# S5 stage of a two-layer decoder: output weights completed by a transfer that adds, in place of two GpSimd differences

## The reference

```python
lam_bar = exp(lam * dt)                        # one complex number per group and state
b_bar   = (lam_bar - 1) / lam * (b_re + i b_im)
bu      = b_bar applied to 16 channels of u     # per group, 64 states
states[t] = lam_bar * states[t-1] + bu[t]       # over the 512 tokens
y[t]    = Re(states[t]) . c_re - Im(states[t]) . c_im
z       = gelu(y + d * u) @ w_glu + b_glu       # then h += val * sigmoid(gate)
```

## Time and profile before

| | |
|---|---|
| Median of 3 runs | 1032.54 us (1030.46 to 1032.89) |
| Profiled execution, its own time | 1030.94 us |
| Its span | 1029.2 us (1.7 us lie around it) |
| PE busy | 1000.4 us, 97% of the span |
| DVE busy | 828.3 us, 80% |
| ACT busy | 477.1 us, 46% |
| POOL busy | 306.5 us, 30% |
| S5 stage | about 0 to 84.85 us, where TensorE's first GLU product starts |

### The profile page before, as it was taken

The page is one execution under the profiler, slowest core; times in us unless marked ns, Lnnn a source line. Parts: engine busy times, 40 slices in busy tenths (PEclk is TensorE's granted clock), DMA queues, the critical chain, the costliest instruction groups (busy, mean ns, idle before and its releaser), DMA issues.

```text
span 1029.2 us, 16636 instructions
## 1 busy us (share of the span) xinstructions
PE 1000.4 (97%) x5850; PEld 824.2 (80%) x5850; DVE 828.3 (80%) x1147; ACT 477.1 (46%) x872; POOL 306.5 (30%) x256
## 2 busy tenths in 40 slices
PE   9889999999999999999999999998999999999996
PEld 4677888888888888888887766886888888888886
DVE  7993588798898988995985777788898888989845
ACT  7863323444455344543413888236355354544421
POOL 8996887300000000031957320770000000001150
PEclk9899999999999999999999999998999999999999
DMA  6123434122322322230333110241322322234012
GB/s 253 37 44 130 139 106 143 62 91 101 136 75 88 111 113 102 82 123 1 123 128 103 43 61 1 82 163 60 104 82 82 132 92 102 82 104 160 22 42 82
DMA packets 31878, 97.53 MB, mean 95 GB/s; under 512 B 10696, under 2 KB 13256, under 8 KB 27984
## 3 DMA queue, kind: packets, MB, share of 16 engines
q1 hardware_dynamic: 31824, 96.83, 26.8%
HBM read 92.36 MB, written 2.10 MB: 92 GB/s over the span
## 4 chain that ended last, share of the span: by engine, by line
PE 78%; DVE 14%; issue 3%; ACT 2%; POOL 1%; POOLq 0%; DVEq 0%; ACTq 0%
PE ps L1744 17%; PE ps L1747 9%; PE ps L1765 8%; PE ps L1766 8%; PE ps L1767 8%; PE ps L1704 5%; PE ps L1705 5%; PE ps L1706 5%; DVE act L1069 3%; PE ps L1650 1%; PE ps L1652 1%; PE ps L1651 1%; PE ps L1937 1%; PE ps L1912 1%; PE ps L1924 1%
## 5 line engine op out<-in xcount | busy, mean ns | idle before, releaser
L448 POOL TENSOR_TENSOR gate_sb<-gate_sb 128x1 f32<-128x1 f32 x60 | 23.4, 390 | 688.0 <-DMA raw<-panels_in 508.3
L537 POOL TENSOR_TENSOR w_lo<-raw,w_hi 128x1024 fp32r<-128x1024 f32 x60 | 149.4, 2490 | 5.0
L1766 PE MATMUL ps<-hid,w_hi 128*128 128x512 f32 x384 | 150.5, 392 | 0.0
L1765 PE MATMUL ps<-hid,w_hi 128*128 128x512 f32 x384 | 150.4, 392 | 0.0
L1767 PE MATMUL ps<-hid,w_lo 128*128 128x512 f32 x384 | 149.6, 390 | 0.0
L700 ACT ACTIVATE s_hi<-w_raw 128x1024 fp32r<-128x1024 f32 (+1 forms) x104 | 87.8, 844 | 100.1 <-PE ps L1747 93.7
L1744 PE MATMUL ps<-hid,s_hi 128*128 128x512 f32 x448 | 121.3, 392 | 0.6 <-ACT acc L764 0.6
L1704 PE MATMUL ps<-hid,w_hi 128*128 128x512 f32 x304 | 120.4, 396 | 0.0
L1705 PE MATMUL ps<-hid,w_hi 128*128 128x512 f32 x304 | 118.6, 390 | 0.0
L1706 PE MATMUL ps<-hid,w_lo 128*128 128x512 f32 x304 | 118.5, 390 | 0.0
L1179 DVE TENSOR_TENSOR s_lo<-w_raw,s_hi 128x1024 fp32r<-128x1024 f32 (+1 forms) x104 | 101.8, 990 | 18.0 <-ACT s_hi L700 10.6
(11 more groups left out here) (272 smaller groups left out, 2052.4 us busy)
## 6 DMA issues: line engine op xcount, KB each, us to landing
raw<-panels_in SPq DMA_DIRECT2D x108, 512.0 KB, 3.3
w_raw<-pairs_in SPq DMA_DIRECT2D x28, 1024.0 KB, 5.4
xy<-xu_in SPq DMA_DIRECT2D x4, 512.0 KB, 8.1
out<-h SPq DMA_DIRECT2D x8, 256.0 KB, 2.1
prm<-prm_in SPq DMA_DIRECT2D x1, 1280.0 KB, 6.4
h<-x_rows_in SPq DMA_DIRECT2D x1, 1280.0 KB, 13.4
h<-x_rows_in SPq DMA_DIRECT2D x1, 768.0 KB, 7.0
dd<-dd_in SPq DMA_DIRECT2D x1, 256.0 KB, 6.3
```

The lines of the kernel that those rows point to most:

```text
L537: nc.gpsimd.tensor_tensor(w_lo[:, s, :], raw[:, s % 2, :], w_hi[:, s, :].bitcast(F32), ALU.subtract).then_inc(w_split, 1)
L1765: mm(to, w_hi[:, s, w], hid[:, 0, 0, HK * par + k, :], start=(k == 0), stop=False)
L1766: mm(to, w_hi[:, s, w], hid[:, 0, 1, HK * par + k, :], start=False, stop=False)
```

## The change

The real part of `w_ri` was `c_sum*l_re - c_im*l_sum`, the imaginary part `c_re*l_dif - c_sum*l_re`. Now the signs of `l_sum` and `l_dif` are chosen so that both parts are a sum with the same term `c_sum*l_re`, and the imaginary part is negated everywhere (in `w_ri`, `p_ri`, and the rotations of `run_states`). GpSimd writes two of the products straight into `w_ri` and the common one into `w_add` (2 buffers, with zeros at lag 0). Then one transfer, issued from GpSimd with an accumulate operation, adds `w_add` to both parts of `w_ri`, lag 0 included. The product `k_both` goes from VectorE to GpSimd, where `project(o)` makes it along with `k_im`.

```diff
-        w_mul = sb("w_mul", [P, 3, OGP, J + 1, C], where=early)
+        w_add = sb("w_add", [P, 2, OGP, J + 1, C], where=early)
...
-        k_both = sb("k_both", [P, OGP, J, C], where=early)
+        k_both = sb("k_both", [P, 2, OGP, J, C], where=early)
...
             def weights_mul(o, parts=range(3)):
 
-                wait(pool, w_done, 2 * o)
-                factors = ((c_sum, l_re), (PR("c_re"), l_dif), (PR("c_im"), l_sum))
+                wait(pool, y_mm, o - 2)
+                wait(pool, w_done, 16 * (o - 1))
+                w = w_ri[o % 3]
+                factors = ((w_add[:, o % 2], c_sum, l_re), (w[:, 1], PR("c_re"), l_dif), (w[:, 0], PR("c_im"), l_sum))
                 for i in parts:
...
             def weights_sum(o):
+
                 pool.wait_ge(w_part, 3 * o + 3)
-                wait(pool, y_mm, o - 2)
-                for ri, (a, b) in enumerate(((0, 2), (1, 0))):
-                    tt(w_ri[o % 3][:, ri, :, 1:].rearrange("p g j c -> p g (j c)"),
-                       w_mul[:, a, :, 1:].rearrange("p g j c -> p g (j c)"),
-                       w_mul[:, b, :, 1:].rearrange("p g j c -> p g (j c)"), sub).then_inc(w_done, 1)
-
-            def project_im(o):
+                wait(pool, w_lag0, 2 * o + 2)
+                wait(pool, w_done, 16 * o)
+                if o < 2:
+                    wait(pool, zeroed, 5 + o)
+                nc.gpsimd.dma_start(w_ri[o % 3][:].rearrange("p r g j c -> p r (g j c)"),
+                                    w_add[:, o % 2].rearrange("p g j c -> p (g j c)").unsqueeze(1)
+                                    .to_broadcast([P, 2, OGP * (J + 1) * C]), accum_op=add).then_inc(w_done, 16)
+
+            def project(o):
+
                 wait(pool, p_done, 2 * o - 2)
-                tt(k_im[:, o % 2], octet(PR("b_re"), o).unsqueeze(2).to_broadcast([P, OGP, J, C]),
-                   x_dif[:, pairs_of(o), :].unsqueeze(3).to_broadcast([P, OGP, J, C]), mul).then_inc(k_part, 1)
+                for t, b, x in ((k_both, "b_im", x_sum), (k_im, "b_re", x_dif)):
+                    tt(t[:, o % 2], octet(PR(b), o).unsqueeze(2).to_broadcast([P, OGP, J, C]),
+                       x[:, pairs_of(o), :].unsqueeze(3).to_broadcast([P, OGP, J, C]), mul).then_inc(k_part, 1)
...
             weights_mul(0, (0,))
             wait(pool, setup_v, SETUP_X)
-            project_im(0)
-            project_im(1)
+            project(0)
             weights_mul(0, (1, 2))
+            project(1)
             weights_sum(0)
             wait(pool, setup_a, SETUP_RSTD)
             inputs(0)
+            weights_mul(1)
             wait(pool, s_dd, 16)
             tt(dd[:, 0], dd[:, 0], dd[:, 1], mul).then_inc(setup_p, 1)
-            weights_mul(1)
             weights_sum(1)
...
-            for o in range(3, NO):
-                project_im(o)
+            for o in range(2, NO):
+                project(o)
                 weights_mul(o)
+                inputs(o)
                 weights_sum(o)
-                inputs(o)
...
-                    act_fn(w_ri[o % 3][:, ri, :, 0, :], octet(PR(c), o), ACT.Copy, scale=1.0 - 2.0 * ri).then_inc(w_lag0, 1)
+                    act_fn(w_ri[o % 3][:, ri, :, 0, :], octet(PR(c), o), ACT.Copy).then_inc(w_lag0, 1)
...
-                tt(k_both[:], octet(PR("b_im"), o).unsqueeze(2).to_broadcast([P, OGP, J, C]),
-                   xsum_ps[:, pairs_of(o), :].unsqueeze(3).to_broadcast([P, OGP, J, C]), mul).then_inc(p_part, 1)
...
             def project_sum(o):
                 q = o % 2
-                v.wait_ge(p_part, 2 * o + 2)
-                v.wait_ge(k_part, o + 1)
+                v.wait_ge(p_part, o + 1)
+                v.wait_ge(k_part, 2 * o + 2)
...
             def lags(o):
 
-                wait(pe, w_done, 2 * o + 2)
+                wait(pe, w_done, 16 * o + 16)
```

More of the change, by code:

```diff
@@ L154, in build @@
         sb("slots_hi", [P, 2, D], where=early)
-        w_mul = sb("w_mul", [P, 3, OGP, J + 1, C], where=early)
+        w_add = sb("w_add", [P, 2, OGP, J + 1, C], where=early)
+        sb("slots_mid", [P, OGP * (J + 1) * C], where=early)
         turn_k = sb("turn_k", [8, L], where=early)
         turn_t = sb("turn_t", [8, L], where=early)
-        sb("slots_lo", [P, 4 * D - 3 * OGP * (J + 1) * C - 2 * L], where=early)
+        sb("slots_lo", [P, 4 * D - 3 * OGP * (J + 1) * C - 3 * L], where=early)
         k_im = sb("k_im", [P, 2, OGP, J, C], where=early)
-        k_both = sb("k_both", [P, OGP, J, C], where=early)
+        k_both = sb("k_both", [P, 2, OGP, J, C], where=early)
         rs = sb("rs", [P, 2, OGP, NK], where=early)
@@ L207, in build @@
         x_dif = sb("x_dif", [P, GP, J], where=s5)
+        x_sum = sb("x_sum", [P, GP, J], where=s5)
         rstd_u = sb("rstd_u", [P, 2, NK], where=s5)
@@ L324, in build @@
         tanh_ps = ps[:, 4, 288:352].rearrange("p (n g) -> p n g", g=GP)
-        xsum_ps, xre_ps = (ps[:, 5, a:a + GP * J].rearrange("p (g n) -> p g n", n=J) for a in (0, 256))
+        xre_ps = ps[:, 5, 256:256 + GP * J].rearrange("p (g n) -> p g n", n=J)
         ident, ones = C_("ident"), C_("ones")
@@ L452, in weights_mul @@
             def weights_mul(o, parts=range(3)):
[L454 to L455 removed]
+                wait(pool, y_mm, o - 2)
+                wait(pool, w_done, 16 * (o - 1))
+                w = w_ri[o % 3]
+                factors = ((w_add[:, o % 2], c_sum, l_re), (w[:, 1], PR("c_re"), l_dif), (w[:, 0], PR("c_im"), l_sum))
                 for i in parts:
[L457 to L458 removed]
+                    to, c, l = factors[i]
+                    tt(to[:, :, 1:], octet(c, o).unsqueeze(2).to_broadcast([P, OGP, J, C]),
                        l[:, pairs_of(o), 1:].unsqueeze(3).to_broadcast([P, OGP, J, C]), mul).then_inc(w_part, 1)
@@ L484, in _ @@
             nc.gpsimd.memset(decay[:, :, 0:1], 0.0).then_inc(zeroed, 1)
+            for i in range(2):
+                nc.gpsimd.memset(w_add[:, i, :, 0], 0.0).then_inc(zeroed, 1)
             wait(pool, setup_v, SETUP_INV)
@@ L515, in _ @@
             nc.gpsimd.tensor_scalar(minus[:], ident, -1.0, 0.0, mul, add).then_inc(negated, 1)
-            project_im(2)
-            weights_mul(2)
-            weights_sum(2)
-            inputs(2)
-            for o in range(3, NO):
-                project_im(o)
+            for o in range(2, NO):
+                project(o)
                 weights_mul(o)
+                inputs(o)
                 weights_sum(o)
-                inputs(o)
-            wait(pool, w_done, 2 * NO)
             def split(u):
@@ L541, in _ @@
             split(1)
+            wait(pool, w_done, 16 * NO)
             wait(pool, p_done, 2 * NO)
@@ L918, in _ @@
             link(tt(l_re[:], cos_l[:], mag_ps, mul))
-            link(tt(l_sum[:], l_re[:], lim_ps, add))
-            link(tt(l_dif[:], l_re[:], lim_ps, sub))
+            link(stt(l_sum[:], l_re[:], -1.0, lim_ps, mul, sub))
+            link(tt(l_dif[:], lim_ps, l_re[:], sub))
             assert count[0] == SETUP_L
@@ L949, in _ @@
             link(tt(x_im[:], xa_ps[:, 1], x_tmp[:, 1], add))
-            link(tt(x_dif[:], x_im[:], xre_ps, sub))
+            link(tt(x_dif[:], xre_ps, x_im[:], sub))
+            link(tt(x_sum[:], xre_ps, x_im[:], add))
             assert count[0] == SETUP_X
-            link(tt(xsum_ps, xre_ps, x_im[:], add))
             def products(o):
@@ L976, in row @@
                     return t.rearrange("p g j c -> p (g j c)")
-                tt(row(p_ri[:, q, 0]), products(o), row(k_both[:]), sub).then_inc(p_done, 1)
-                tt(row(p_ri[:, q, 1]), products(o), row(k_im[:, q]), add).then_inc(p_done, 1)
+                tt(row(p_ri[:, q, 0]), products(o), row(k_both[:, q]), sub).then_inc(p_done, 1)
+                tt(row(p_ri[:, q, 1]), row(k_im[:, q]), products(o), sub).then_inc(p_done, 1)
             def mean_square():
@@ L1009, in run_states @@
                 v.wait_ge(rot, 8 * o + 2)
-                tt(b[:, 0], b[:, 0], turn[:, 1], add).then_inc(rot, 1)
-                tt(b[:, 1], b[:, 1], turn[:, 0], sub).then_inc(rot, 1)
+                tt(b[:, 0], b[:, 0], turn[:, 1], sub).then_inc(rot, 1)
+                tt(b[:, 1], b[:, 1], turn[:, 0], add).then_inc(rot, 1)
                 wait(v, decayed, 1)
```

8 lines of the change are left out of this document (3 added, 5 removed).

## The result

The changed kernel takes 1061.13 us (median of 4 runs: 1058.13, 1058.68, 1063.59, 1064.14) against 1031.5 us of the kernel before, measured beside it (1030.16 to 1032.89). The ratio is 1.0289, with a 95% interval of 1.0254 to 1.0325. I had forecast 1044.5 us in a range of 1036 to 1056: the direction was right, the size was less than half of what came (+12.8 us forecast, +29.6 us measured), and the time lies above the range. The profiled execution took 1058.13 us, with a span of 1056.3 us.

A forecast was written before the change was run, and what follows sets the result against it. VectorE and nearly full GpSimd paced the S5 stage; the transfer's loop would replace them. Start +3.2 us and turns of 9.55 us put the first GLU product at 97.7 for 84.85, +12.8 us: 1044.5 us, range 1036 to 1056.

The forecast's parts named there:

- The loop: S5 stage: lags through ACT's lag-0 copies 4.35 us, hop 0.1, transfer 5.1; octets 9.55 us apart, over 8.00.
- my 97.7: End of the S5 stage: forecast start in us of TensorE's first GLU product, 84.85 before, so +12.8 us.
- VectorE and GpSimd cost nothing more: S5 stage: VectorE's octet 7.4 us and GpSimd's 7.0 with the issue, both waiting for TensorE; splits ready early.
- Start, 44.9 for the lags of octet 2: Stage start: lags of octet 1 at 31.9 us, +3.2, kept by packed ACT to octet 2, 41.69 + 3.2.
- T: Accumulating transfer, start of issue to landing: taken as 5.1 us, counted six times (octets 1 and 3 to 7).
- Octet 3: Before octet 3's transfer: lag-0 copies end 3.8 us after octet 2's lags start, at 48.7, then a 0.1 us hop.
- The upper bound, 5.9: Longest time allowed for the transfer: 1152 KB by the loads' rows, 5.9 us; would add 4.8 us, to 1049.
- The hop of 0.1 us: In each turn, between the end of ACT's lag-0 copies and the transfer: some 0.1 us.
- Full clock at 0.60: Main case: turns at full TensorE clock, transfer of 3.5 to 6 us, 1036 to 1050 us, at 1044.5; chance 0.60.
- a falling clock at 0.22: Rival: TensorE's clock falls in some octets' waits of 2.7 us, 1048 to 1059 us; chance 0.22.
- a turn at the lower level at 2.9 us: TensorE's lags, sums and `turn_y` at 1.2 GHz, each about 0.95 us longer: 2.9 us more per turn.
- its own time of 1059: Clock falling in all five turns: +14 us, 1059; within the case of chance 0.22.

The follow-up runs named there:

- e11: Changed kernel with GpSimd additions instead of the transfer for octets 0 and 1, `dd` before octet 1's products, its `project` behind them; 1059.19 us, ratio 1.0273.
- e5: Changed kernel with a plain copy in place of the accumulating transfer, output not the reference's; 1048.13 us (1 run).
- e6: Changed kernel with the accumulating transfer over the first part of `w_ri` only, 288 KB, output not the reference's; 1050.77 us (1 run).
- e3: Changed kernel with seven idle fp32 products on TensorE ahead of each wait for the transfer in octets 3 to 7; 1057.56 us, ratio 1.0273.
- e2: Changed kernel without the transfer: GpSimd adds `w_add` to both parts of `w_ri` itself, `k_both` stays on GpSimd; 1041.69 us, ratio 1.0106.
- e7: Changed kernel with ACT's lag-0 copies of octet o + 2 made right behind the activation of octet o - 1; 1039.66 us, ratio 1.0112.
- e1: Changed kernel with the product `k_both` back on VectorE, the transfer kept; 1067.89 us, ratio 1.0357.

## Why the prediction was wrong

The loop, its place and the direction held; the size didn't, and the step that cost most was to take the full clock for granted in the waits. The first GLU product came 20.0 us later than my 97.7. By the prediction's steps:

- **VectorE and GpSimd cost nothing more.** Right. VectorE lost `k_both` and waits for TensorE's sums, 29.6 us in six octets (I had said about 2 us each; it is 4.9, because the turns are longer). GpSimd's splits were ready, its second one at 112.5 us.
- **Start, 44.9 for the lags of octet 2: measured 49.14, +4.2 us.** This step failed, besides that of the clock below. I took the lags of octet 1 as the first place where the start is late. But the lags of octet 0 are late already, at 27.52 for 23.63: their transfer lands at 26.3 and `dd`, moved behind three products on GpSimd, is ready at 27.4. Behind them on TensorE stand `turns(2)`, `fold(1)` and `turns(3)`, which feed ACT and VectorE. They came late and at the lower clock, and the lags of octet 1 began 2.1 us after their own transfer had landed. So T, which I counted once here, wasn't the last wait at octet 1. I named what queues behind the transfer on GpSimd, and not what queues behind the lags on TensorE. e11, with neither the transfer nor the late `dd`, starts the lags of octet 2 at 44.85; the share of each is open.
- **Octet 3: from the lags of octet 2 to the issue I had 3.9 us, measured 5.06: +1.2 us.**
- **T = 5.1: mis-sized.** The five transfers in the loop took 6.73, 5.82, 5.33, 5.87 and 5.81 us, and 0.04 us from landing to the lags: +4.3 us in sum. The upper bound, 5.9, held for four of them. By the estimate from e5 and e6 the accumulation costs 2.6 times the bytes of a copy, not twice.
- **The hop of 0.1 us: measured 0.54,** from the end of ACT's copy to the issue. A turn at full clock in e3 is 4.69 us up to the issue where I had 4.45; four turns, +0.9 us.
- **Full clock at 0.60, a falling clock at 0.22: this is the step that failed, and the largest one.** From lags to issue the four turns took 6.22, 6.93, 5.99 and 6.79 us; with 4.68 each at full clock, as in e3, 7.2 us of the loop are the clock's. Another 2.2 us lie between the lags of octet 7 and the GLU (7.81 us for the 5.6 forecast). I had priced a turn at the lower level at 2.9 us, of which 1.3 to 2.3 came, since the level rose again within the turn. The evidence against it was one stretch with 2.93 us of waits in 20, spread over many short gaps. The evidence for it was the fall after a single wait of 0.82 us, in a place thin with work. The new waits are one gap of 3.8 to 5.3 us in each turn, and I had compared sums of idle time. That the length of the single gap decides isn't shown, and it can't be all: the lags of octet 6 in e2 kept 1.09 us after a gap of 2.12 us, those of octet 1 in the kernel before were slow after 0.82 us. What is shown is the price: with the same loop and the waits filled, e3 needs 4.68 us in three of four turns where after needed 5.99 to 6.93.

These make 4.2 + 1.2 + 4.3 + 0.9 + 7.2 + 2.2 = 20.0 us. The errors fed each other: a longer transfer means a longer gap in each turn, behind these gaps the clock was low, and the low clock makes the turn longer. The forecast added a turn's parts as if they were independent, and gave the clock as a rival of its own, with its own time of 1059, in place of a consequence of the forecast itself. That rival's time came near, but by other terms: it had neither the late start nor the longer T in it.

The median then stands 29.6 us above before and not 32.9 us, because of the tails described above. The prediction had TensorE at work without a pause and at full clock from the GLU on; the wait at 701.76 us and the low clock behind it, before the change, show that it isn't so everywhere. Two small things in its start: its terms for the second issue add up to 26.7 and not 26.8 us, which changes nothing, and the 14.89 us for the first product came without a source (measured: 14.93).

What stays open: which part of a transfer's 5.3 to 7.3 us is contention with the Toeplitz copies (no run leaves them out), how the late start divides between the transfer and `dd`, which gaps let the clock fall, and where 2 of the 4.3 us of e11's start went.

## What to carry to other kernels

When an edit puts an asynchronous operation between two engines, first write down the loop that closes over it, with everything that must be done before it can start. Here the moment of the start mattered more than the duration: moving two small copies ahead (e7) gained 19.3 us at the first GLU product with the same transfer, and a transfer shorter by 2.2 us (e5) gained 15.0.

If the sum gives TensorE a new wait in each turn, don't leave the clock to the rivals: price the turn at the lower level within the forecast as well. And list what stands behind a waiting instruction on every engine that waits, not only on the one that was edited.

## What the runs showed of the hardware

- An accumulating transfer within SBUF, issued by GpSimd, took 5.8 us for 576 KB and 4.0 us for 288 KB; a plain copy of 576 KB issued in the same way took 3.6 us.
- Its issue is listed with 1.20 to 1.98 us on GpSimd, but the next instruction there starts 0.77 to 1.0 us after it.
- Small copies that SyncE issues while it runs land late: 24 KB in 4.4 us for 1.9.
- One VectorE product with both operands in SBUF was listed with 12.27 us beside a busy GpSimd (e1), where the next ones took 0.69 us.
- With products on idle data (3.19 us) that ended 0.86 to 2.81 us before each wait was over, the granted clock was 1.00 from 61.28 to 94.60 us, and the first GLU product came 6.13 us earlier for doing them:

```profile
61.28:94.60 33.32, 27.94 (x465) 24.56 (x465) 21.80 (x39) 15.37 (x36) 22.55 (x22) 1.00 0.45 82
```
